# Attention scores in three passes, with the keys' low parts made from the bank of transposes

## The reference

```
dq, dk = rope(rms_norm(dq, g_qn)), rope(rms_norm(dk, g_kn))      # 128 wide, per map
s = einsum('bqhmd,bkhmd->bhmqk', q, k) * DA_DK ** -0.5           # prompt: block-causal mask of 64-row chunks
p = softmax(s, axis=-1)
a = p[:, :, 0] - lam * p[:, :, 1]
o = einsum('bhqk,bkhe->bqhe', a, v)                              # then rms_norm and a gain
```

## Time and profile before

| | |
|---|---|
| time, median of 3 runs | 2214.58 us (2214.34 to 2214.62) |
| the profiled execution | 2214.51 us; span in the trace 2212.7 us |
| TensorE busy | 2199.8 us (99%) |
| VectorE, ScalarE, GpSimd busy | 1092.3, 704.6, 666.0 us |
| share of DMA, mean | 99 GB/s |
| granted TensorE clock | 1.00 of full speed, the 2.4 GHz level |

### The profile page before, as it was taken

The page is one execution under the profiler, slowest core; times in us unless marked ns, Lnnn a source line. Parts: engine busy times, 40 slices in busy tenths (PEclk is TensorE's granted clock), DMA queues, the critical chain, the costliest instruction groups (busy, mean ns, idle before and its releaser), DMA issues.

```text
span 2212.7 us, 34135 instructions
## 1 busy us (share of the span) xinstructions
PE 2199.8 (99%) x13064; PEld 2085.8 (94%) x13064; DVE 1092.3 (49%) x2076; ACT 704.6 (32%) x1654; POOL 666.0 (30%) x368
## 2 busy tenths in 40 slices
PE   8999999999999999999999999999999999999999
PEld 8999877789898898998999999999999999999999
DVE  5311544455645456354145568676666663313432
ACT  5200333335555555555221131101111013434311
POOL 4522210230220400403152353233322226476420
PEclk9999999999999999999999999999999999999999
DMA  8622222230130400404751322222122226656311
GB/s 256 193 96 83 72 70 87 78 104 27 56 88 29 117 25 26 123 27 146 241 181 59 110 79 70 68 68 75 59 77 67 68 76 200 184 167 201 93 50 50
DMA packets 312669, 218.18 MB, mean 99 GB/s; under 512 B 16332, under 2 KB 303679, under 8 KB 312544
## 3 DMA queue, kind: packets, MB, share of 16 engines
q1 hardware_dynamic: 219802, 117.33, 18.3%
q10 hardware_dynamic: 92742, 99.15, 13.4%
HBM read 160.15 MB, written 56.29 MB: 98 GB/s over the span
## 4 chain that ended last, share of the span: by engine, by line
PE 98%; DVE 1%; ACT 0%; DMA 0%; issue 0%; ACTq 0%; DVEq 0%
PE ps L639 28%; PE ps L641 28%; PE ps L640 28%; PE ps L918 3%; PE ps L891 3%; PE ps L766 1%; PE ps L767 1%; PE ps L909 1%; PE ps L837 1%; PE ps L842 1%; PE ps L1053 1%; PE ps L839 1%; PE ps L894 0%; PE ps L855 0%; PE ps L1069 0%; PE ps L821 0%
## 5 line engine op out<-in xcount | busy, mean ns | idle before, releaser
L639 PE MATMUL ps<-a_hi,w_hi 128*128 128x352 f32 x2920 | 946.8, 324 | 0.0
L641 PE MATMUL ps<-a_hi,w_lo 128*128 128x352 f32 x2920 | 936.4, 321 | 0.0
L640 PE MATMUL ps<-a_lo,w_hi 128*128 128x352 f32 x2920 | 936.2, 321 | 0.0
L537 POOL TENSOR_SCALAR w_hi<-w_raw 128x1024 fp32r<-128x1024 f32 x150 | 162.9, 1086 | 1408.6 <-PE ps L641 659.1
L639 PEld LDWEIGHTS ps<-a_hi,w_hi 128*128 128x128 f32 x2920 | 547.8, 188 | 3.4 <-issue 2.7
L640 PEld LDWEIGHTS ps<-a_lo,w_hi 128*128 128x128 f32 x2920 | 548.8, 188 | 0.4
L641 PEld LDWEIGHTS ps<-a_hi,w_lo 128*128 128x128 f32 x2920 | 548.2, 188 | 0.0
L539 POOL TENSOR_TENSOR w_lo<-w_raw,w_hi 128x1024 fp32r<-128x1024 f32 x150 | 363.4, 2423 | 12.5
L639 PE MATMUL ps<-w_hi,a_hi 128*128 128x384 f32 (+1 forms) x768 | 283.3, 369 | 0.0
L641 PE MATMUL ps<-w_hi,a_lo 128*128 128x384 f32 (+1 forms) x768 | 273.3, 356 | 0.0
L640 PE MATMUL ps<-w_lo,a_hi 128*128 128x384 f32 (+1 forms) x768 | 273.0, 355 | 0.0
(11 more groups left out here) (228 smaller groups left out, 2522.9 us busy)
## 6 DMA issues: line engine op xcount, KB each, us to landing
w_raw<-w_in SPq DMA_DIRECT2D x64, 512.0 KB, 4.3
w_raw<-w_down SPq DMA_DIRECT2D x48, 512.0 KB, 3.9
w_raw<-w_up SPq DMA_DIRECT2D x44, 512.0 KB, 3.8
hid_d<-scr ACTq DMA_DIRECT2D x22, 512.0 KB, 2.6
w_raw<-w_down SPq DMA_DIRECT2D x24, 384.0 KB, 3.4
scr<-gates_d ACTq DMA_DIRECT2D x24, 352.0 KB, 6.3
gates_d<-full ACTq DMA_DIRECT2D x13, 528.0 KB, 2.6
xt_d<-full ACTq DMA_DIRECT2D x1, 4224.0 KB
```

The lines of the kernel that those rows point to most:

```text
L537: pool.tensor_scalar(hi, raw, 1.0, 0.0, ALU.mult, ALU.add).then_inc(S["w_hi_done"], 1)
L639: pe.matmul(out, lhs[0], rhs[0], start=start, stop=False)
L640: pe.matmul(out, lhs[0], rhs[1], start=False, stop=False)
L641: return pe.matmul(out, lhs[1], rhs[0], start=False, stop=stop)
```

## The change

The score products become three passes. ScalarE takes the high parts of queries and keys out of bank 4, VectorE the low ones. The keys' low parts of the prompt live in weight slot 7 (the `w_hi` half for map 0, the `w_lo` half for map 1), so the second gate's weights move to slot 6, which the B projection uses as well, and the splits on GpSimd get other waits. The sample's low parts lie behind the cached keys' buffer. The cached keys' high part is made by ScalarE, the low part by VectorE a place later than the copy was. Two of the sample's operand pairs move into the matrix of ones, which is set again later. The double buffer of the queries goes.

```diff
-DIFF_GATE_SLOTS = (3, 7)
+DIFF_GATE_SLOTS = (3, 6)
+KEY_SLOT = 7
...
+        q_hi, q_lo = (nc.alloc_sbuf_tensor_at(name, [P, 2, P], F32R, offset=scr_at + 4 * (q_at + n * 2 * P))
+                      for n, name in enumerate(("q_hi", "q_lo")))
+        k_hi = nc.alloc_sbuf_tensor_at("k_hi", [P, 2, NT + PAST], F32R, offset=full_at + 4 * k_t_at)
+        k_lo_last = nc.alloc_sbuf_tensor_at("k_lo_last", [P, 2, NS + PAST], F32R, offset=full_at + 4 * kc_at)
+        k_lo = (w_hi[:, KEY_SLOT, :], w_lo[:, KEY_SLOT, :])
...
         @block.gpsimd
...
                 for j in range(3):
+                    if h and PB_SLOT + j == DIFF_GATE_SLOTS[1]:
+                        wait_piece(pool, h - 1, 5, S["gate_part"])
                     split(0, unit + 3 + j, PB_SLOT + j)
                 for j in range(2):
-                    if h:
-                        wait_piece(pool, h - 1, 4 + j, S["gate_part"])
+                    if j:
+                        pool.wait_ge(S["pb_done"], (h + 1) * TILES)
+                    elif h:
+                        wait_piece(pool, h - 1, 4, S["gate_part"])
...
         @block.tensor
...
-                    last = pe.matmul(ps[0:r, score_bank(m, i) + b // 512, 0:n], q_t[:, i % 2, m, 0:r],
-                                     k_t[:, m, first + b:first + b + n], start=True, stop=not diag)
+                    high = k_hi[:, m, first + b:first + b + n]
+                    low = k_lo[m][:, b:b + n] if i < LAST else k_lo_last[:, m, :]
+                    last = three(ps[0:r, score_bank(m, i) + b // 512, 0:n], (q_hi[:, m, 0:r], q_lo[:, m, 0:r]),
+                                 (high, low), True, not diag)
...
         @block.scalar
...
-            act.dma_start(mask[0:1, 0:P], t["c_mask"][:, 0:P]).then_inc(S["head_const"], 16)
-            act.dma_start(mask[0:1, P + P // 2:2 * P], t["c_mask"][:, P + P // 2:2 * P]).then_inc(S["head_const"], 16)
+            act.dma_start(mask[0:1, :], t["c_mask"]).then_inc(S["head_const"], 16)
...
+                cached = fill_at(s, 0)
+                if cached and cached[1] == 0:
+                    act.wait_ge(S["dc_tr"], cached[0] + 1)
+                    act.activation(k_hi[:, :, NT:NT + PAST], ps[:, 2, 0:2 * P].rearrange("p (m n) -> p m n", m=2),
+                                   ACT.Copy).then_inc(S["xs_done"], 1)
...
                                    accum_out=st[0:r, 29 + 2 * b:30 + 2 * b]).then_inc(S["e1_done"], 1)
                 if turned:
                     h, i, n = turned
+                    r = rows(i)
+                    act.wait_ge(S["d_tr"], n + 1)
+                    if n >= 1:
+                        act.wait_ge(S["s1_done"], n)
+                    v4 = ps[:, 4, :].rearrange("p (m n) -> p m n", m=4)
+                    act.activation(q_hi[:, :, 0:r], v4[:, 0:2, 0:r], ACT.Copy)
+                    act.activation(k_hi[:, :, i * P:i * P + r], v4[:, 2:4, 0:r], ACT.Copy).then_inc(S["xs_done"], 1)
+                if turned:
...
         @block.vector
...
-                dve.tensor_copy(q_t[:, b, :, 0:r], v4[:, 0:2, 0:r]).then_inc(S["d_ev"], 1)
-                dve.tensor_copy(k_t[:, :, i * P:i * P + r], v4[:, 2:4, 0:r]).then_inc(S["d_ev"], 1)
+                dve.tensor_tensor(q_lo[:, :, 0:r], v4[:, 0:2, 0:r], q_hi[:, :, 0:r].bitcast(F32),
+                                  ALU.subtract).then_inc(S["d_ev"], 1)
+                at = slice(i * P, i * P + r)
+                if i < LAST:
+                    for m in range(2):
+                        last = dve.tensor_tensor(k_lo[m][:, at], v4[:, 2 + m, :], k_hi[:, m, at].bitcast(F32),
+                                                 ALU.subtract)
+                else:
+                    last = dve.tensor_tensor(k_lo_last[:, :, 0:NS], v4[:, 2:4, 0:r], k_hi[:, :, at].bitcast(F32),
+                                             ALU.subtract)
+                last.then_inc(S["d_ev"], 1)
...
-                now = fill_at(s, 0)
-                if now and now[1] == 0:
-                    h = now[0]
-                    dve.wait_ge(S["dc_tr"], h + 1)
-                    dve.tensor_copy(k_t[:, :, NT:NT + PAST],
-                                    ps[:, 2, 0:2 * P].rearrange("p (m n) -> p m n", m=2)).then_inc(S["dc_ev"], 1)
                 if weighed:
...
+                now = fill_at(s, 0)
+                if now and now[1] == 0:
+                    h = now[0]
+                    dve.wait_ge(S["xs_done"], cache_parts(h))
+                    dve.tensor_tensor(k_lo_last[:, :, NS:NS + PAST], ps[:, 2, 0:2 * P].rearrange("p (m n) -> p m n", m=2),
+                                      k_hi[:, :, NT:NT + PAST].bitcast(F32), ALU.subtract).then_inc(S["dc_ev"], 1)
...
+            dve.wait_ge(S["pb_done"], RET_TILES)
+            dve.memset(ones[:, :], 1.0)
```

More of the change, by code:

```diff
@@ L134, in kernel_program @@
         ident = sb("ident", [P, P])
+        ones_at = -(-nc.sbuf_base // 32) * 32
         ones = sb("ones", [P, P])
@@ L237, in kernel_program @@
         gqk = f.take(2 * P).rearrange("p (g c) -> p g c", g=2)
-        mask_at = f.at
         mask = f.take(2 * P)
         k_t_at = f.at
-        k_t = f.take(2 * (NT + PAST)).rearrange("p (m n) -> p m n", m=2)
+        f.take(2 * (NT + PAST))
         v_tok = f.take((TILES + 1) * DV).rearrange("p (t c) -> p t c", t=TILES + 1)
@@ L245, in kernel_program @@
         a_t = f.take(1024).rearrange("p (b n) -> p b n", b=8)
+        kc_at = f.at
         kc = f.take(2 * P)
+        f.take(2 * NS)
         rope_b = s.take(512)
@@ L251, in kernel_program @@
         a_w = s.take(1024)
-        q_t = s.take(2 * 2 * P).rearrange("p (b m n) -> p b m n", b=2, m=2)
+        q_at = s.at
+        s.take(2 * 2 * P)
         o_n = s.take(2 * DV).rearrange("p (b n) -> p b n", b=2)
@@ L255, in kernel_program, with key_parts, cache_parts @@
         st = s.take(48)
+        q_hi, q_lo = (nc.alloc_sbuf_tensor_at(name, [P, 2, P], F32R, offset=scr_at + 4 * (q_at + n * 2 * P))
[3 more added lines that the diff above has]
+        k_lo = (w_hi[:, KEY_SLOT, :], w_lo[:, KEY_SLOT, :])
+        def key_parts(h, i):
+            return TILES + 9 + (TILES + 1) * h + i + 1 + (i == LAST)
+        def cache_parts(h):
+            return TILES + 9 + (TILES + 1) * h + LAST + 1
         def sample_pair(name, at, n):
             return nc.alloc_sbuf_tensor_at(name, [P, n, 2, NS], F32R, offset=at)
-        pair_at = ((full_at + 4 * f.at, 3), (scr_at + 4 * s.at, 2), (u_last_at + 4 * 12 * 4, 2),
-                   (full_at + 4 * (mask_at + P), 1))
-        assert f.at + 3 * 2 * NS <= KT * NT and s.at + 2 * 2 * NS <= 6 * UW
+        pair_at = ((full_at + 4 * f.at, 2), (scr_at + 4 * s.at, 2), (u_last_at + 4 * 12 * 4, 2), (ones_at, 2))
+        assert f.at + 2 * 2 * NS <= KT * NT and s.at + 2 * 2 * NS <= 6 * UW
         pairs = [sample_pair(f"pair{j}", at, n) for j, (at, n) in enumerate(pair_at)]
-        pair_k0 = (0, 3, 5, 7)
+        pair_k0 = (0, 2, 4, 6)
         def pair(k):
@@ L588, in _ @@
                     pool.wait_ge(S["pb_done"], HEADS * TILES)
+                if j == KEY_SLOT:
+                    pool.wait_ge(S["s1_done"], HEADS * TILES)
                 split(U_B, j, j)
@@ L1522, in _ @@
                                    accum_out=st[0:r, 29 + 2 * b:30 + 2 * b]).then_inc(S["e1_done"], 1)
+                if turned:
+                    h, i, n = turned
+                    r = rows(i)
[5 more added lines that the diff above has]
+                    act.activation(k_hi[:, :, i * P:i * P + r], v4[:, 2:4, 0:r], ACT.Copy).then_inc(S["xs_done"], 1)
                 if turned:
@@ L1824, in _ @@
             dve.scalar_tensor_tensor(neg_lam, lamt[:, 7:8], LAM_INIT, lamt[:, 6:7], ALU.subtract, ALU.subtract).then_inc(S["lam_d"], 1)
-            dve.wait_ge(S["head_const"], 6 * 16)
+            dve.wait_ge(S["head_const"], 5 * 16)
             dve.tensor_scalar(gqk[:, 0, :], gqk[:, 0, :], DK ** -0.5, None, ALU.mult).then_inc(S["g_scaled"], 1)
@@ L1970, in operands @@
                 r, b = rows(i), i % 2
-                dve.wait_ge(S["d_tr"], n + 1)
-                if freed(i, n) > 0:
-                    dve.wait_ge(S["s1_done"], freed(i, n))
+                dve.wait_ge(S["xs_done"], key_parts(h, i))
                 v4 = ps[:, 4, :].rearrange("p (m n) -> p m n", m=4)
-                dve.tensor_copy(q_t[:, b, :, 0:r], v4[:, 0:2, 0:r]).then_inc(S["d_ev"], 1)
-                dve.tensor_copy(k_t[:, :, i * P:i * P + r], v4[:, 2:4, 0:r]).then_inc(S["d_ev"], 1)
+                dve.tensor_tensor(q_lo[:, :, 0:r], v4[:, 0:2, 0:r], q_hi[:, :, 0:r].bitcast(F32),
[9 more added lines that the diff above has]
+                last.then_inc(S["d_ev"], 1)
             def inverse_of_sum(h, i, n):
```

## The result

The changed kernel took 2217.61 us in the median of 22 runs, the kernel before 2214.42 in 22 beside them: 3.2 us more, ratio 1.0015 (95% interval 1.0009 to 1.0021). Forecast were 2218.1 and a change inside 0.2%; the measured change is inside it too.

The account below looks back on a forecast made before the run. TensorE's own work was taken as nearly all of the chain of waits. Waits of (0.67 + 0.45 + 2.58) x 4 heads = 14.8 less a saving of 11.2 gave 2214.5 + 3.6 = 2218.1 us; range 2206 to 2228, likeliest case 2213 to 2223.

Parts of the forecast that it names:

- saving of the passes: TensorE's score products: three split passes cost less than float32, 63.9 us down to 51.4; 11.2 saved (10.0 to 12.5).
- waits for the exponential: Second scores of tiles 4 to 7 wait for map 0's exponential, late behind ScalarE's table load: 2.58 us per head.
- waits for operands and mix: First scores wait for split operands, 0.67 us per head; transposes wait for VectorE's mix in tiles 0 to 3, 0.45.
- net: Whole kernel: waits of 14.8 us less the saving of 11.2, 3.6 more, inside 0.2%.
- the estimate from the Trainium skill: TensorE's 128-column pass, held by its weight load at 0.107 us, would make the saving 10.1 instead of 11.2.
- The chain's score line: Sign in the profile page's chain of waits: the score line at some 52 to 54 us if the forecast is right.
- D: End of the four transposes that turn a tile; the forecast counts later starts in us from it.
- the wake: Time from a ScalarE result to the waiting TensorE pass: taken as 0.25 us, with 0.04 as low bound.
- The rest: GpSimd's weight splits, SP's loads, mask transfer, reset of the ones, cached keys' low part: all put at nothing.
- The hidden load: Rival: ScalarE's table load still runs in free time, exponentials in time; 10.3 us less, 2207.8; chance 0.12.
- All covered: Rival: operand chain under D + 1.41 and table load hidden, only the saving left: 2203.3 us; chance 0.06.
- The port: Rival: GpSimd's second-gate subtraction starts first and holds VectorE's mix and operands, up to 2.38 per head: 2227.6; chance 0.14.

Follow-up runs that it names:

- experiment 6: 4 with all four high and low parts on VectorE and the square-root table load ahead of the fold copy: 2203.09 us, ratio 0.9952 to the kernel before.
- experiment 1: Changed kernel with the square-root table load moved ahead of ScalarE's high copies: 2208.86 us, ratio 0.9980 to the kernel before.
- 4: Changed kernel with three moves: table load ahead of copies, operand wait split by pass, mix ahead of operands in all tiles: 2202.70 us, ratio 0.9953.
- experiment 3: Kernel before, float32 scores kept, with three unused ScalarE copies waiting for the transposes ahead of the table load: 2220.44 us, ratio 1.0027.
- 4 to 6: 4, experiment 6 and the run between: 4 with all four parts on VectorE and ScalarE's old order, 2202.19 us, ratio 0.9951.
- the second alone: Changed kernel with only TensorE's operand wait split by pass, the key's low part last: 2216.53 us, ratio 1.0012 to the kernel before.

## Why the prediction was right

| step | forecast, us | measured, between |
|---|---|---|
| saving of the passes | 11.2 | 11.2 (before to 6) |
| waits for the exponential | 10.3 | 7.6 (after to 1), and 0.7 left until 6 |
| waits for operands and mix | 4.5 | 5.9 (1 to 4) |
| net | 3.6 | 2.9 |

The mechanism is the one forecast; that the net comes so near is in part luck, since the term for the exponential was 2.0 too large and that for operands and mix 1.4 too small.

**The saving.** The total holds, its parts less so. A pass takes, start to start, 0.11, 0.12, 0.18 and 0.23 for 128, 256, 384 and 512 columns. TensorE at tile 4 of after, the tail of 128:

```profile
539.05 0.22 PE L663 MATMUL ps<-k_hi,q_hi 128*128 128x128 f32 x1
539.11 0.27 PE L664 MATMUL ps<-w_hi,q_hi 128*128 128x128 f32 x1
539.22 0.28 PE L665 MATMUL ps<-k_hi,q_lo 128*128 128x128 f32 x1
539.33 0.38 PE L920 MATMUL ps<-full 128*128 128x64 f32 x2
```

I took 0.085 for 128; it is 0.11, my upper bound, and the mask product behind it gets slower as well (0.11 to the next for 0.06). There the estimate from the Trainium skill (TensorE: Matmul & The Clock Gate, section LDWEIGHTS: 0.107) was nearer, and 128 columns in three passes are dearer than the float32 product of 0.22. Its total of 10.1 is still not the measured one: the sample tile gave back the difference. From the start of the last transpose before it to what follows it, it went from 0.59 us to 0.33, where proportion gave 0.05 less. That 11.2 met 11.2 is in part luck: by the starts of before and of experiment 6, the products with 128-column passes came out some 1.2 dearer than forecast and the sample tile some 1.7 cheaper. The sample's passes also speak for the width of the weights as what holds a 128-column pass: they stream 160 columns over weights of 32 columns and take 0.075 each, less than 128 columns over weights of 128. The chain's score line, which I named as a sign, can't be read alone: L663 to L665 are the lines of every split product.

**The exponential.** The step with the largest term was right in kind and in its chain: D + 2.12 for 2.11, D + 6.71 for 6.72, the load behind the copies. That holds in tiles 3 to 6, and not "in every tile": in tiles 0 to 2 the exponential comes at D + 5.35 to 5.91, and no second product waits for it. Mis-sized is the wake, the time from a result to the start of what waits for it: taken as 0.25 and measured as 0.14 (572.07 to 572.21). Of that, 0.09 is the read of the accumulator, which ends that much after the exponential's row; from its end to the pass are 0.05, near the 0.04 taken as the low bound, and the same at tile 6 of experiment 3. Why L1358 to L837 took 0.25 stays open. With 0.14 the forecast's own sums give 0.73, 1.27, 0.13 and 0.01 for tiles 6, 7, 4 and 5; measured, up to the second pass and against the rows with no wait, 0.71, 1.26, some 0.05 and none. So close a match is partly luck: the measured times hold 0.1 of weight load that the forecast has not, and in tile 7 the exponential came at D + 8.95 (9.08 forecast) and TensorE asked 0.10 earlier too. I had 0.14 within my bounds and took the only row at hand. The bound itself is mis-added: a wake of 0.04 takes 3.0 away and not 3.4, since tile 5 had only 0.12 to lose.

**Operands and mix.** The wait of 0.20 in tiles 0 to 2 is there (0.17 to 0.19), and 0.06 in tile 6; at tile 1 the first pass starts at D + 1.60, with 1.61 forecast. Missed was that a pass that waited also shows its weight load, 0.10 more. It comes in tiles 0 to 2 and 6, and as 0.07 in tiles 3 to 5, whose lead of 1.62 was just the length of the chain (1.61) and no reserve. By the starts up to the second pass, tiles 0 to 6 lose 0.29, 0.29, 0.28, 0.07, 0.08, 0.07 and 0.15: 1.23 a head, not 0.67; the mix, whose reader came that much later, cost 0.16 instead of 0.45.

**The rest and the rivals.** No projection waited for GpSimd. The hidden load (2207.8) did not happen, since the diff puts the load behind the copies; experiment 1, which hides it, took 2208.86. All covered (2203.3) is where 4 to 6 stand, 2202 to 2203. The port decided by which starts first, as said: the mix by 0.28.

## What to carry to other kernels

When work is put on an engine that has time to spare, ask what that idle time is hiding: here it hid a table load that waited for nothing, and an instruction that waits for another engine, put ahead of it, took the cover away. Put what waits for nothing ahead of what waits. And when a wait is taken out, look at the next one behind it: here three moves gave 13.5 us together, and the second alone 1.1.

## What the runs showed of the hardware

- A float32r pass that had to wait takes about 0.10 us longer than one in a row (0.34 for 0.23 at 512 columns, 0.22 for 0.12 at 256); the float32 product after a wait lost as much in experiment 3.
- The pace of a pass is in proportion from 256 columns up (0.45 ns a column) and stays at 0.11 us for 128; with weights of 32 columns a pass of 160 takes 0.075.
- Shared access goes both ways: GpSimd's rounding was held to 1.78 by a mix that started before it, and a one-column VectorE instruction to 1.41 by GpSimd's subtraction.
- A TensorE pass that waits for an exponential with a sum starts 0.05 us after the end of the accumulator's read on ScalarE, which ends 0.09 after the exponential's own row (572.07, 572.16 and 572.21 at tile 6; the same in experiment 3).
